# Retention stage of a decoder step: loop written out, gate weight units through both weight buffers, split one unit ahead

## The reference, cut to what matters

```python
qa, ka, va, qr, kr, vr, gr = mixer_project(rms_norm(hp, g_mix[l]), w_in[l])
att_o, wk, wv = window_attention_prompt(qa, ka, va, attn_sinks[l])
ret_o, rs = retention_prompt(qr, kr, vr)          # 8 chunks of 128 tokens, 4 heads, state carried
hp = hp + mixer_merge(att_o, ret_o, gr, ...)      # GroupNorm(ret_o) * silu(gr), then @ w_out
```

## Time and profile before

| | us |
|---|---|
| median of three runs | 1683.91 (1682.66 to 1684.43) |
| the profiled execution, its own time | 1683.8 |
| its span, first to last instruction | 1681.9 |
| PE busy (9950 matmuls) | 1573.4 |
| DVE busy | 646.8 |
| ACT busy | 444.4 |
| POOL busy | 259.1 |

### The profile page before, as it was taken

One profiled execution on the slowest core, in us unless ns is written; L12 is line 12 of the kernel. 1 busy time (PEld: TensorE's weight loads), 2 busy tenths in 40 slices (PEclk: granted clock), 3 DMA queues, 4 the chain that ended last, 5 costly groups with the idle time before them and its releaser, 6 DMA issues.

```text
span 1681.9 us, 25382 instructions
## 1 busy us (share of the span) xinstructions
PE 1573.4 (94%) x9950; PEld 1498.7 (89%) x9950; DVE 646.8 (38%) x1169; ACT 444.4 (26%) x780; POOL 259.1 (15%) x312
## 2 busy tenths in 40 slices
PE   5969999989869989988999999999999999999998
PEld 5869777768859989877889899999999999999998
DVE  3542455535554452233326533233322332233222
ACT  3530233323231211033214332113201331123212
POOL 2010100013226530011256000000000000000043
PEclk9979899999969999999999999999999999999999
DMA  6751000010133131102553111111111111111112
GB/s 182 205 192 50 26 26 26 13 35 26 38 102 133 39 97 41 38 1 100 191 193 105 51 50 45 43 51 39 49 50 45 43 50 50 38 50 41 47 38 103
DMA packets 152615, 115.33 MB, mean 69 GB/s; under 512 B 12880, under 2 KB 141968, under 8 KB 152272
## 3 DMA queue, kind: packets, MB, share of 16 engines
q1 hardware_dynamic: 140816, 72.49, 15.1%
q0 software_dynamic: 10576, 37.66, 6.4%
q10 hardware_dynamic: 1152, 4.19, 0.7%
HBM read 101.19 MB, written 14.16 MB: 69 GB/s over the span
## 4 chain that ended last, share of the span: by engine, by line
PE 78%; issue 11%; DVE 5%; DMA 2%; ACT 2%; POOL 1%; DVEq 0%; SPq 0%; ACTq 0%; POOLq 0%
PE ps L353 21%; PE ps L354 21%; PE ps L355 21%; PE ps L1047 4%; PE ps L1112 2%; PE ps L1323 2%; PE ps L1341 2%; PE ps L1129 2%; DMA raw<-in_w_xv 1%; DVE wlo L342 1%; DVE xlo L1470 1%; ACT whi L326 1%; DMA raw<-in_w_xk 1%; PE ps L1187 0%; PE ps L1189 0%
## 5 line engine op out<-in xcount | busy, mean ns | idle before, releaser
L353 PE MATMUL ps<-xhi,whi 128*128 128x352 f32 x1392 | 458.6, 329 | 16.2 <-DVE wlo L342 9.0
L354 PE MATMUL ps<-xlo,whi 128*128 128x352 f32 x1392 | 450.8, 324 | 0.0
L355 PE MATMUL ps<-xhi,wlo 128*128 128x352 f32 x1392 | 450.6, 324 | 0.0
L353 PE MATMUL ps<-yhi,whi 128*128 128x352 f32 x1152 | 375.0, 326 | 6.0 <-DVE xq L1490 1.9
L354 PE MATMUL ps<-ylo,whi 128*128 128x352 f32 x1152 | 370.9, 322 | 0.0
L355 PE MATMUL ps<-yhi,wlo 128*128 128x352 f32 x1152 | 370.6, 322 | 0.0
L353 PEld LDWEIGHTS ps<-xhi,whi 128*128 128x128 f32 x1392 | 265.3, 191 | 28.4 <-issue 17.3
L354 PEld LDWEIGHTS ps<-xlo,whi 128*128 128x128 f32 x1392 | 265.7, 191 | 0.1
L355 PEld LDWEIGHTS ps<-xhi,wlo 128*128 128x128 f32 x1392 | 264.8, 190 | 0.0
L326 ACT ACTIVATE whi<-raw 128x1024 fp32r<-128x1024 f32 x126 | 132.9, 1055 | 429.8 <-PE ps L355 397.2
L353 PEld LDWEIGHTS ps<-yhi,whi 128*128 128x128 f32 x1152 | 217.4, 189 | 9.0 <-DVE wlo L342 2.9
(11 more groups left out here) (273 smaller groups left out, 1417.3 us busy)
## 6 DMA issues: line engine op xcount, KB each, us to landing
raw<-in_w_up SPq DMA_DIRECT2D x32, 512.0 KB
raw<-in_w_down SPq DMA_DIRECT2D x32, 512.0 KB
raw<-in_w_xo SPq DMA_DIRECT2D x16, 512.0 KB
kx<-in_cache_mem_k POOLq DMA_DIRECT2D x16, 512.0 KB, 4.6
raw<-in_w_in SPq DMA_DIRECT2D x14, 512.0 KB, 3.8
spill<-hT POOLq DMA_DIRECT2D x8, 528.0 KB, 6.2
hT<-spill POOLq DMA_DIRECT2D x8, 528.0 KB, 5.4
raw<-in_w_xk SPq DMA_DIRECT2D x8, 512.0 KB
```

The source lines that it names most:

```text
L353: pe.matmul(out, whi[:, q, k, :], x1, start=k == 0, stop=False)
L354: pe.matmul(out, whi[:, q, k, :], x2, start=False, stop=False)
L355: mm = pe.matmul(out, wlo[:, q, k, :], x1, start=False, stop=k == KB - 1)
```

## The change

The retention passes are written out on ACT, PE and DVE (POOL keeps its loop). The gate units become an ordinary continuation of the stream: they alternate between both buffers, are loaded by `load_unit`, and are split one unit ahead. The split of the first gate unit moves into the last window step; that of gate unit n2+1 into step p = 0 of pass n2, on ACT behind `ret_v`, on DVE behind `onrm`; the split of the first `w_out` unit moves from behind the stage into its last pass. `product` takes the alternating banks with its usual wait (the default of `before`). The waits of TensorE for `s_wlo` stay.

```diff
-        def load_single(sp, u, u0, loaded, src):
-            wait(sp, s_wlo, u)
-            sp.dma_start(raw[:, 0], src).then_inc(loaded, 16)
-        def split_single(act, u, u0, loaded):
-            act.wait_ge(loaded, (u - u0) * 16 + 16)
-            act.wait_ge(s_mm, chunks_before(u))
-            act.activation(whi[:, 0], raw[:, 0], ACT.Copy).then_inc(s_whi, 1)
...
-            stream(wi[:, :, 4 * P:], U_IN + 4, 10)
-            single(U_GATE, 4, s_raw1, wi[:, :, (U_GATE - U_IN) * P:])
+            stream(wi[:, :, 4 * P:], U_IN + 4, 14)
...
@@ ACT, win
-                    if not end:
-                        split_hi(act, n + U_RET + 1, 1 - p)
+                    split_hi(act, n + U_RET + 1, 1 - p)
@@ ACT, ret
+                    if n < NQ - 1:
+                        ret_v(n + 1)
                     if p == 0:
-                        split_single(act, n2 + U_GATE, U_GATE, s_raw1)
-                    if not (isinstance(n, int) and n == NQ - 1):
-                        ret_v(n + 1)
+                        split_hi(act, n2 + U_GATE + 1, 1 - n2 % 2)
...
-            Steps(act, s_act).loop(0, NQ // 2 - 1, ret)
-            ret(NQ // 2 - 1)
+            for n2 in range(NQ // 2):
+                ret(n2)
             silu(RH - 1)
             act.wait_ge(s_mm, chunks_before(U_OUT))
-            split_hi(act, U_OUT, 0)
@@ PE, ret
-                    product(pe, u, 0, p, xhi, xlo, CW, before=0)
+                    product(pe, u, q, p, xhi, xlo, CW)
...
-                product(pe, u, 0, 2, xhi, xlo, CW)
+                product(pe, u, q, 2, xhi, xlo, CW)
...
-            Steps(pe, s_act).loop(0, NQ // 2 - 1, ret)
-            ret(NQ // 2 - 1)
+            for n2 in range(NQ // 2):
+                ret(n2)
@@ DVE, win
-                    if not end:
-                        split_lo(dve, u + 1, 1 - p)
+                    split_lo(dve, u + 1, 1 - p)
@@ DVE, ret
-                    if p == 0:
-                        split_lo(dve, u, 0)
-                    if not (isinstance(n, int) and n == NQ - 1):
+                    if n < NQ - 1:
                         ret_keys(n + 1)
...
                         dve.tensor_scalar(onrm[:, h, :], ...).then_inc(s_ron, 1)
+                    if p == 0:
+                        split_lo(dve, u + 1, 1 - n2 % 2)
...
-                        scaled(za, U_IN + 8)(u, 0, c).then_inc(s_ev, 1)
+                        scaled(za, U_IN + 8)(u, n2 % 2, c).then_inc(s_ev, 1)
...
-            st.loop(0, NQ // 2 - 1, ret)
-            ret(NQ // 2 - 1)
-            split_lo(dve, U_OUT, 0)
+            for n2 in range(NQ // 2):
+                ret(n2)
```

More of the change, by code:

```diff
@@ L307, in layer @@
         s_raw = [S("raw_loaded_even"), S("raw_loaded_odd")]
-        s_raw1 = S("gate_raw_loaded")
         s_whi, s_wlo = S("w_hi_made"), S("w_lo_made")
@@ L840, in ret @@
                     n = n2 * 2 + p
+                    if n < NQ - 1:
+                        ret_v(n + 1)
                     if p == 0:
-                        split_single(act, n2 + U_GATE, U_GATE, s_raw1)
-                    if not (isinstance(n, int) and n == NQ - 1):
-                        ret_v(n + 1)
-                    if p == 0 and not (isinstance(n, int) and n == 0):
+                        split_hi(act, n2 + U_GATE + 1, 1 - n2 % 2)
+                    if p == 0 and n > 0:
                         silu(n2 - 1)
@@ L1176, in ret @@
             def ret(n2):
-                u = n2 + U_GATE
+                u, q = n2 + U_GATE, n2 % 2
                 for p in range(2):
                     n = n2 * 2 + p
-                    end = isinstance(n, int) and n == NQ - 1
+                    end = n == NQ - 1
                     pe.wait_ge(s_rin, n * 2 + 2)
```

## The result

| | before | after |
|---|---|---|
| median, us | 1683.91 (1682.66 to 1684.78, 5 runs) | 1661.41 (1659.12 to 1667.42, 5 runs) |
| span of the profiled execution, us | 1681.9 | 1659.4 |
| last gate evacuation starts, us | 468.29 | 455.61 |
| `kvtok` starts, us | 472.06 | 456.70 |
| from `kvtok` to the end of the span, us | 1209.8 | 1202.7 |

The ratio is 0.9872 [0.9854, 0.9889]: 22.5 us faster, where 16.2 were forecast. The prediction of 1667.7 had the direction, and the mechanism in the stage that was changed, but its range began at 1664.5, 3.1 us above the result. The last two lines of the table say where to look: the stage that was changed, and the 1200 us behind it that were not.

The account below looks back on a forecast made before the run. The prediction took TensorE as the bound, with its waits for DVE's low split in even retention steps and the lower clock behind them as savable: 13.6 + 2.6 = 16.2 us off, giving 1667.7 us, range 1664.5 to 1672.5.

Parts of the forecast that it names:

- The wait in the even steps: Retention, scores to turning: even steps fall to the odd step's 4.58 us, saving 13.6, about 9 wait and 4.6 clock.
- What is late next: Even retention steps: with POOL's power at 1.01, onrm starts 1.30 behind the variance and ends 0.35 us ahead of TensorE.
- The other end of the bound: Even retention steps: with POOL's power kept at 1.94, onrm ends 0.6 us late in each of four passes, 2.4 in all.
- The edits costed at nothing: Moved splits on DVE and ACT, loads, first gate unit's split in the last window step, writing out: each cost 0.
- The `w_out` unit: Behind the retention stage: without the two splits there, kvtok starts earlier, gain 2.6 us, bounds 0 and 3.3.
- later stages are driven by events, so the shift should reach the end: Everything behind retention: the whole 16.2 us gained upstream was to arrive at the end of the kernel.
- The range: Whole kernel: 1664.5 to 1672.5 us, taking in rivals that lose part of the gain, and 3 us below the forecast.

Follow-up runs that it names:

- fill_wait: Kernel before, with 14 useless matmuls put into TensorE's wait for the low weight part in each even step: 1679.52 us, 0.9966 of before.
- split_before_keys: Kernel after, with DVE's low split, still one unit ahead, back between the statistics and the keys of the next step: 1668.1 us, 0.9906 of before.
- undo_wout: Kernel after, with the first w_out unit split behind the retention stage again, on ACT and DVE: 1670.67 us, 0.9908 of before.
- after_late3: Kernel after, with the copy to kvtok made three more times, a delay of about 1.35 us: 1668.97 us, 0.9914 of before.
- after_late6: Kernel after, with the copy to kvtok made six more times, a delay of about 2.7 us: 1671.4 us, 0.9927 of before.

## Why the prediction was wrong, and where it was right

- *The wait in the even steps:* right. 4.57 us per step against 4.58, and 13.67 for the four passes against 13.6. The split into 9 of waiting and 4.6 of clock was borne out by `fill_wait`, which gained 4.6 (4.4 of it in the stage of its profile) and kept the wait's time.
- *What is late next:* right for the kernel after. POOL's power came out at 1.01 and `onrm` at 1.29 behind the variance. The other end of the bound, the power at 1.94, was priced too low: 0.6 in each pass and 2.4 in all, where `split_before_keys` measured 0.8 and, over the stage, 3.4. The sum let `onrm` start at 403.1, where the earlier trace rows has it at 403.23 behind that same power. In `split_before_keys` the power takes 1.96 beside the split, and 1.01 in the kernel after; in the kernel after the split takes 1.71 beside the staging, where 1.23 was its length. Each time the one that starts second is longer, by somewhat less than the first still had to run (0.95 of 1.08, and 0.48 of 0.63). The Trainium skill, "SBUF — State Buffer" (SBUF: two separate sides), says that of a VectorE instruction with two SBUF inputs and a GpSimd instruction that reads SBUF, whichever starts first has the shared ports for the whole instruction and the other blocks; the runs come near that both ways.
- *The edits costed at nothing:* right. The split behind `onrm` leaves DVE 0.67 idle, in the window step the statistics' wait is 0.67 where it was 0.92, ACT's affine part begins on TensorE's turning as before, and writing out measured 0.9998 [0.9984, 1.0012].
- *The `w_out` unit:* right, 2.68 against 2.6, shown by the after trace and by `undo_wout`; the 35.4 us to the first product of `w_out` did not change.
- *The step that failed* is the one sentence that carried the sum to the end: "later stages are driven by events, so the shift should reach the end". It treats the 1210 us behind the stage as a constant. They are not one, even without any change: 1209.8 in one profile of the kernel before, 1200.1 in another, with the same waits in both. The clock that TensorE has after a wait of 2 to 4 us is not given by the wait. Not the waits but the time at 0.50 behind them differs, 20.5 us before and 6.8 after. The missing term is 7.1 us in the profiled pair, and 5 to 6 by the medians (1683.91 less 1661.41 or, over nine runs, 1662.39, less 16.35).
- *The range* went 3.2 us below the forecast, with the clock of the sample part as one of the reasons, and had no room for falls behind it. The trace of before could have given it some. The page's row of the granted clock has a 9 in every slice from 505 us on, which is 90% or more and hides the falls, and the windows that the prediction goes by lie in the retention stage. Those behind it add up to 20.47 us at 0.50, so that up to about 10 us, an estimate, could come out there by no merit of the change. A range reaching 10 below the 1667.7 would have held the result.

What is shown: the excess lies behind `kvtok`, goes with the time at 0.50 there and not with which kernel it is, and the kernel before reaches such times unaided in 2 of 13 runs, one of them profiled without a fall. What stays open is why the kernel after has few falls in both of its profiles, and the kernel before, by its times, only in few of its runs. A small delay brings the falls to the kernel after (`after_late3`, `after_late6`, `undo_wout`), but the 3.4 us of `split_before_keys` did not in its profile, and my rule for which delays do was wrong twice. So these 5 to 7 us belong to this arrangement and can't be counted as earned by the moved splits; they can be lost to any later edit upstream, as `undo_wout` lost 5.6 for 2.68.

## What to carry to other kernels

Split a weight one unit ahead even where the engines look idle: the price of a short wait of TensorE can be the wait plus the chunk that runs at the lower clock behind it (three of four passes here), and a timeline from one fixed instruction to another shows both in one number. Choose the new place by what runs beside it on POOL, since the same subtraction was free behind `onrm` and cost 0.8 us a pass ahead of the keys. And when a shift of some microseconds meets a later stage with waits of 2 to 4 us, give the range room for the clock there, and judge an edit by its own stage before crediting it with the total.

## What the runs showed of the hardware

In 13 runs, one program on one core has two groups of times, 1674 and 1682 to 1686, with a granted clock of 0.972 and 0.973 against 0.963 to 0.967: the clock after one and the same wait of 3.6 us was 0.50 in one execution and 1.00 in another. The Trainium skill, "TensorE: Matmul & The Clock Gate" (Part 1: The HAM clock gate), says of a kernel's start that the count of matmuls at the lower clock varies from run to run, and puts the penalty under 1% of a typical span. Here the same is seen behind waits in the middle of the kernel, and the size agrees: 9.7 us of 1682 are 0.58%. That is over a third of what the change brought.

Adding work can save time: 14 useless matmuls in each of four waits made the kernel before 0.9966 [0.9954, 0.9979] of its time. And in the kernel after, a delay of 1.35 us on one engine cost 6.6 by the medians.
